# Prompt attention of a hybrid decoder step: values stationary, scaled probabilities, output by feature, and the order of scaling and maximum

## The reference

```
s = q . k * SCALE, masked;  p = softmax(s);  o_branch = p @ v          (for each of the 3 branches)
attn = g0 * o_compressed + g1 * o_selected + g2 * o_window             (gates g per row, branch and head)
merged = concat(rmsnorm(o_rnn) * gn_rnn, rmsnorm(attn) * gn_attn)      (rmsnorm over 512 features)
x = x + mods2 * (merged @ w_out);  then norm, SwiGLU feed-forward, norm
```

## Time and profile before

| | |
|---|---|
| Median of three timed runs | 1877.02 us (1874.16 to 1878.92) |
| Profiled execution, its own time | 1875.1 us |
| Its span in the trace | 1873.3 us |
| TensorE busy (weight loads) | 1721.3 us (1546.4) |
| VectorE busy | 938.1 us |
| ScalarE busy | 751.4 us |
| Mean granted clock of TensorE | 0.94 |

### The profile page before, as it was taken

The page is one execution under the profiler, slowest core; times in us unless marked ns, Lnnn a source line. Parts: engine busy times, 40 slices in busy tenths (PEclk is TensorE's granted clock), DMA queues, the critical chain, the costliest instruction groups (busy, mean ns, idle before and its releaser), DMA issues. The chain is left out here.

```text
span 1873.3 us, 30402 instructions
## 1 busy us (share of the span) xinstructions
PE 1721.3 (92%) x11011; PEld 1546.4 (83%) x11011; DVE 938.1 (50%) x1733; ACT 751.4 (40%) x1187; POOL 302.1 (16%) x303
## 2 busy tenths in 40 slices
PE   6999979799969899897679979999999999999998
PEld 3988945478859787785459979999999999999997
DVE  3647662344466666674555724443445443444433
ACT  3435501134446555462333435432235432345322
POOL 1100033311030000000015503003305013100032
PEclk7999989989979898898789989999999999999999
DMA  8355320164300000104525555544554544555443
GB/s 288 108 147 169 92 73 23 59 197 144 111 6 2 1 1 0 51 0 197 226 58 155 145 167 135 137 112 139 152 138 132 155 125 134 153 135 152 127 140 93
DMA packets 297157, 214.47 MB, mean 114 GB/s; under 512 B 20382, under 2 KB 284366, under 8 KB 293807
## 3 DMA queue, kind: packets, MB, share of 16 engines
q1 hardware_dynamic: 290412, 172.61, 32.3%
q0 software_dynamic: 4816, 40.73, 5.8%
q10 hardware_dynamic: 1842, 0.05, 0.1%
HBM read 206.07 MB, written 11.41 MB: 116 GB/s over the span
## 5 line engine op out<-in xcount | busy, mean ns | idle before, releaser
L423 DVE TENSOR_TENSOR ff_lo<-ff_raw,ff_hi 128x2048 fp32r<-128x2048 f32 (+1 forms) x126 | 265.6, 2108 | 220.1 <-ACT ff_hi L419 220.1
L428 PE MATMUL banks<-low_rows,ff_hi 128*128 128x352 f32 x1120 | 360.2, 322 | 0.0
L427 PE MATMUL banks<-ff_h_hi,ff_hi 128*128 128x352 f32 x1056 | 342.8, 325 | 12.3 <-DVE ff_lo L423 12.3
L429 PE MATMUL banks<-ff_h_hi,ff_lo 128*128 128x352 f32 x1056 | 340.1, 322 | 0.0
L419 ACT ACTIVATE ff_hi<-ff_raw 128x2048 fp32r<-128x2048 f32 (+1 forms) x126 | 215.4, 1710 | 235.5 <-PE banks L429 220.2
L428 PEld LDWEIGHTS banks<-low_rows,ff_hi 128*128 128x128 f32 x1120 | 211.5, 189 | 0.3
L427 PEld LDWEIGHTS banks<-ff_h_hi,ff_hi 128*128 128x128 f32 x1056 | 199.0, 188 | 13.6 <-issue 13.4
L429 PEld LDWEIGHTS banks<-ff_h_hi,ff_lo 128*128 128x128 f32 x1056 | 199.5, 189 | 0.0
L427 PE MATMUL banks<-hid_hi,ff_hi 128*128 128x352 f32 x528 | 171.9, 326 | 4.4 <-DVE hid_lo L423 4.1
L429 PE MATMUL banks<-hid_hi,ff_lo 128*128 128x352 f32 x528 | 170.6, 323 | 0.0
L428 PE MATMUL banks<-hid_lo,ff_hi 128*128 128x352 f32 x528 | 170.1, 322 | 0.0
(11 more groups left out here) (414 smaller groups left out, 3155.2 us busy)
## 6 DMA issues: line engine op xcount, KB each, us to landing
ff_raw<-in_w_gate SPq DMA_DIRECT2D x66, 512.0 KB, 4.0
ff_raw<-in_w_up SPq DMA_DIRECT2D x66, 512.0 KB, 5.2
ff_raw<-in_w_down SPq DMA_DIRECT2D x48, 384.0 KB, 4.1
late_ada<-in_w_ada SPq DMA_DIRECT2D x16, 1024.0 KB, 5.7
ff_raw<-in_w_down SPq DMA_DIRECT2D x48, 320.0 KB, 3.4
ff_raw<-in_w_out SPq DMA_DIRECT2D x24, 512.0 KB, 5.3
s_raw<-in_w_in SPq DMA_DIRECT2D x48, 128.0 KB, 2.6
streams<-in_x_prompt SPq DMA_DIRECT2D x4, 1024.0 KB, 9.3
```

The costliest lines, as they stand in the source:

```text
L423: return dve.tensor_tensor(lo, raw, hi.bitcast(F32), ALU.subtract)
L427: pe.matmul(out, lhsT=w_hi, rhs=x_hi, start=first, stop=False)
L428: pe.matmul(out, lhsT=w_hi, rhs=x_lo, start=False, stop=False)
L429: return pe.matmul(out, lhsT=w_lo, rhs=x_hi, start=False, stop=last)
```

## The change

- Value products: the values are stationary (64 weight columns), the turned probabilities of 128 rows move. The two key heads' products go to partitions 0 to 63 and 64 to 127 of one PSUM bank. Both branches and the compressed branch accumulate in the same bank.
- For that the probabilities are multiplied by gate over row sum before they are turned (`weigh`), in place, on VectorE. The merges go.
- ScalarE evicts a row tile's sum, features on the partitions, into `attnT` (`take`, two instructions for each row tile and trip).
- VectorE's order in step n is `weigh(n-1)`, `top(n)`, `copy(n-2)`.
- The four trips are one written-out sequence of 128 units; the next trip's staging, compressed scores and gates are issued between units of the trip before. The unit order in a row tile is branch, then key head.
- Four buffers of turned probabilities in place of two.
- GpSimd squares and sums the output by feature in trips 1 and 3; TensorE sums over features. The decode attention loses the squares and the scaling of the rows; it gets eight products of the identity with the row rates. The trunk spreads the rates by eight matmuls, VectorE scales `attnT` with gain and rate, and the turns of eight row tiles go. The output projection takes the gated stream's chunks first, attention's behind.

The core of the diff:

```diff
@@ prompt_attention, VectorE
-                def top(u):                       # step u: top(u), copy(u - 2), merge(u - 3)
-                def merge(u):
-                    t, h, br = units[u]
-                    j = slice(u % 4, u % 4 + 1)
-                    dve.wait_ge(probs_ready, i * U + u + 1)
-                    s.then(dve.reciprocal(coef[:, j], den[:, j]))
-                    s.then(dve.tensor_tensor(coef[:, j], coef[:, j], gsel[:, t, br, h:h + 1], ALU.mult))
-                    dve.wait_ge(out_summed, i * U + u + 1)
-                    dve.scalar_tensor_tensor(out, ps[6 + u % 2][:, 0:HEAD_DIM], coef[:, j], out, ALU.mult, ALU.add
-                                             ).then_inc(merged, 1)
+            def weigh(n):
+                i, t, br, h = order[n]
+                j = slice(n % 4, n % 4 + 1)
+                w = len(tiles_of[n]) * P
+                dve.wait_ge(probs_ready, n + 1)
+                s.then(dve.reciprocal(coef[:, j], den[:, j]))
+                s.then(dve.tensor_tensor(coef[:, j], coef[:, j], gsel[i % 2][:, t, br, h:h + 1], ALU.mult))
+                dve.tensor_scalar(probs[n % 2][:, 0:w], probs[n % 2][:, 0:w], coef[:, j], None, ALU.mult).then_inc(scaled, 1)
+            for n in range(1, DONE):
+                i, u = trip_of(n)
+                if n - 1 < N:
+                    weigh(n - 1)
+                if n < N:
+                    top(n)
+                if 0 <= n - 2 < N:
+                    copy(n - 2)
+                if i + 1 < KA:
+                    if u == SHIFT_AT:             # 4
+                        compress_shift(i + 1)
+                        pick_gates(i + 1)
+                    if u == PROBS_AT:             # 6
+                        compress_weigh(i + 1)
+                    if u == COPY_AT:              # 10
+                        compress_copy(i + 1)
+                    if u == FIRST_HALF_AT:        # 19
+                        stage(i + 1, 0)
+                if 0 < i < KA and u == SECOND_HALF_AT:   # 3
+                    stage(i, 1)
@@ prompt_attention, ScalarE
+            def exp(n):
+                act.wait_ge(max_ready, n + 1)
+                if n >= 2:
+                    act.wait_ge(turned0, n - 1)
+                    if second[n - 2]:
+                        act.wait_ge(turned1, upto[n - 2])
+                w = len(tiles_of[n]) * P
+                if n >= 4:
+                    act.wait_ge(scaled, n - 3)
+                act.activation(probs[n % 2][:, 0:w], psum[:, place[n]:place[n] + w], ACT.Exp,
+                               bias=nmax[:, n % 4:n % 4 + 1], accum_out=den[:, n % 4:n % 4 + 1]).then_inc(probs_ready, 1)
+            def take(v):
+                i, t, _, _ = order[2 * v]
+                act.wait_ge(out_summed, v + 1)
+                for h in range(N_KV):
+                    head = i + h * GROUP
+                    act.activation(attnT[own[head % 2], head // 2, t * P:(t + 1) * P], ps[6 + t % 2][own[h], 0:P], ACT.Copy
+                                   ).then_inc(taken, 1)
@@ prompt_attention, TensorE (turn(n) now waits for scaled instead of probs_ready)
-                        m = pe.matmul(ps[6 + u % 2][:, 0:HEAD_DIM], lhsT=pT[u % 2][:, j * P:(j + 1) * P],
-                                      rhs=kvn[:, kt, col:col + HEAD_DIM], start=(j == 0), stop=(j == len(tiles_of[u]) - 1))
+                for j, kt in enumerate(tiles):
+                    for h in range(N_KV):
+                        col = 2 * KV_WIDTH * br + KV_WIDTH + h * HEAD_DIM
+                        m = pe.matmul(bank[own[h], 0:P], lhsT=kvn[:, kt, col:col + HEAD_DIM], rhs=pT[(2 * v + h) % 4][:, j, :],
+                                      start=False, stop=(br == 2 and j == len(tiles) - 1), skip_group_check=True)
+            for n in range(2, DONE):              # step n: qk(n), turn(n - 2), weighted((n - 4) // 2) if n is even
@@ sample_attention, group 0
-                    for t in range(TILES):
-                        s.then(act.activation(win[:, 0:ATTN_WIDTH], attn[:, t, :], ACT.Square, accum_out=attn_sum[:, t:t + 1]))
-                    for t in range(TILES):
-                        s.done(dve.scalar_tensor_tensor(attn[:, t, :], attn[:, t, :], attn_sum[:, t:t + 1], gain_row, ALU.mult, ALU.mult))
@@ sample_attention, group 1
+                    for t in range(TILES):
+                        s.done(dve.tensor_scalar(rate_rows[:, t, :], ident[:, :], attn_sum[:, t:t + 1], None, ALU.mult))
@@ trunk
-            for t in range(4):
-                turn(t)
+            for t in range(TILES):
+                m = pe.matmul(ps[RATE_BANKS[t // 4]][:, t % 4 * P:(t % 4 + 1) * P], lhsT=ones[:, :], rhs=rate_rows[:, t, :], start=True, stop=True)
+            def scale(g):                         # VectorE: g = 0 first of all, 1 and 2 between the blocks
+                dve.wait_ge(rates_spread, 1)
+                ...
+                            m = dve.scalar_tensor_tensor(rows, rows, V["gn_attn"][:, c:c + 1], ps[RATE_BANKS[x // 512]][:, x % 512:x % 512 + y - x],
+                                                         ALU.mult, ALU.mult)
```

More of the change, by code:

```diff
@@ L1324, in prompt_attention @@
     second = [len(x) > 4 for x in tiles_of]
-    upto = [sum(second[:u + 1]) for u in range(U)]
-    C1 = upto[-1]
-    HT = TILES // 2
+    upto = [sum(second[:u + 1]) for u in range(N)]
+    HQ = SEQ // 2
+    DONE = N + 4
+    CMP_AT, SHIFT_AT, EXP_AT, PROBS_AT, TURN_AT, COPY_AT = 3, 4, 4, 6, 9, 10
+    FIRST_HALF_AT = PER // 2 + 3
+    SECOND_HALF_AT = 3
     with ExitStack() as st:
@@ L1489, in _, with double @@
+            for t in range(TILES):
+                pe.wait_ge(squared, t + 1)
+                m = pe.matmul(ps[4][:, 2 * t:2 * t + 2], lhsT=acc[:, t * P:(t + 1) * P], rhs=ones[:, 0:2], start=True, stop=True)
+            m.then_inc(rows_summed, 1)
         @block.scalar
         def _(act):
+            def double(i, half):
+                cols = slice(half * HQ, (half + 1) * HQ)
+                for h in range(N_KV):
+                    act.wait_ge(q_hi_done, (i * 2 + half) * N_KV + h + 1)
+                    act.activation(QD[h][own[1 - h], cols], QD[h][own[h], cols].bitcast(F32), ACT.Copy).then_inc(q_doubled, 1)
@@ new lines, in _ @@
+            double(0, 0)
+            compress_exp(0)
+            double(0, 1)
+            for n in range(DONE + 1):
+                i, u = trip_of(n)
+                if 0 <= n - 2 < N:
+                    copy(n - 2)
+                if n < N:
+                    exp(n)
+                if n < N and u == EXP_AT and i + 1 < KA:
+                    compress_exp(i + 1)
+                if n < N and u == FIRST_HALF_AT and i + 1 < KA:
+                    double(i + 1, 0)
+                if n < N and u == SECOND_HALF_AT and i:
+                    double(i, 1)
+                if n % 2 == 1 and n >= 5 and order[n - 5][2] == 2:
+                    take((n - 5) // 2)
@@ new lines, in _ @@
+            s.then(dve.memset(ck_pair[:, :, :], 0.0))
+            for h in range(N_KV):
+                s.done(dve.memset(QL[h][own[1 - h], :].bitcast(F32), 0.0))
+                s.done(dve.tensor_scalar(ck_pair[own[h], h, :], ck_p[own[h], :], SCALE, None, ALU.mult))
+            s.fence()
+            dve.wait_ge(masks_loaded, 48)
+            for dst, src in ((diag_b, diag), (tail_b, tail), (ident_b, ident)):
+                dve.tensor_copy(dst[:, :], src[:, :]).then_inc(masks_cast, 1)
+            stage(0, 0)
@@ L2421, in _ @@
             hi(0, 2, 8, 2 * KD)
-            for p in order[8:]:
-                part(p)
+            part(NG)
             hi(0, 2, 9, 2 * KD)
@@ L2556, in _ @@
                 dve.sem_inc(sem, 2)
+            scale(0)
             lo(0, 2, 0, 2 * KD)
-            for p in order[0:5]:
-                part(p)
+            part(0)
+            scale(1)
             lo(0, 2, 1, 2 * KD)
@@ L2571, in _ @@
             lo(0, 2, 5, 2 * KD)
-            part(order[7])
+            part(2)
             take(4)
```

469 lines of the change are left out of this document (234 added, 235 removed).

## The result

The changed kernel takes 1887.39 us, the median of five runs (1881.05 to 1891.71); the kernel before took 1875.50 beside it (1873.85 to 1878.92, five runs). The forecast had put the change at 21 us above the kernel before (1898 against 1877); it is 12. The profiled execution is the longest of the five: 1891.71 us with a span of 1889.9, against a span of 1873.3 before.

A forecast was written before the change was run, and what follows sets the result against it. TensorE bounded the old steady part, waits the trip borders; afterwards a closed VectorE-ScalarE chain would bound the prompt attention. 1875.1 + 26.9 (stage) - 6 (decode attention) + 0 (trunk) = 1896.0, with 1.9 carried over 1898 us; range 1881 to 1920.

The forecast's parts named there:

- the ring: Prompt attention, VectorE and ScalarE: maximum, exponential, scaling, next maximum as one closed chain, 317.8 us over 128 units.
- start of the chain: Prompt attention's first maximum: same VectorE work before or just behind it, so the chain begins where it did, 546.3.
- gap from maximum to exponential: Handover from VectorE's maximum to ScalarE's exponential in each unit: fixed 0.15 us, from 0.16 in the earlier trace.
- all else from maximum to maximum: Work laid into the chain: next trips' preparation 15.2 us, GpSimd's squares touching VectorE 1 us (0 to 6).
- decode attention: Row scaling gone, second group starts 8.7 us sooner, gather takes part back: 6 us saved (3 to 8.7).
- trunk: Start of the trunk: up to 2 us later, fewer turns give back up to 2; zero, within 2.
- rival A: Prompt attention: chain shorter per unit than summed, level at 0.17 us less, 1860 at 0.3 less; chance 0.12.
- Preparation: Between units on VectorE: shift and gates, weighing, staging in halves; 5.1 us unhidden, three times, 15.2 us.
- TensorE's work: Prompt attention: some 60 us of value products leave; about 50 us a trip remain, 65 at the dear bound.
- rival C: Value products not side by side: 232 ns a pair, TensorE 65 us a trip, time unchanged; no chance of its own.
- Rival B: Prompt attention: TensorE's clock falls through short rests and TensorE becomes the bound, 1930 us; chance 0.13.
- The carry-over: Whole kernel: timed runs' median lay 1.9 us above the profiled run; added again, 1896.0 becomes 1898.

The follow-up runs named there:

- no_scaling: Changed kernel without VectorE's scaling of the probabilities, the turn waiting for the coefficient instead (output lacks gate and normalisation): 1832.6 us, ratio 0.9772.
- before_act_unrolled: Kernel before, with ScalarE's prompt-attention program written out in place of its hardware loop over the trips: 1875.5 us, ratio 1.0004.
- both_orders: Changed kernel with VectorE's next maximum ahead of the scaling and TensorE's value products behind the next scores, ahead of the turn: 1832.2 us, ratio 0.9770.
- the edit alone: Kernel before, without squares and scaling of seven of the eight prompt row tiles in the decode attention: 1871.2 us, ratio 0.9984.

## Why the prediction was right, and where its sizes were off

By its own sum, in us:

| step | forecast | measured |
|---|---|---|
| the ring sets the pace | yes | yes: waits and timeline; no_scaling -54.8 |
| start of the chain | 546.3 | 544.8 |
| gap from maximum to exponential, 128 times | 0.15 each, 19.2 | 0.03 in 124 of them, as 128: 3.8, so 15.4 too many |
| all else from maximum to maximum (preparation, GpSimd) | 16.2 | 22.8 |
| from the last scaling to the stage's end | 5 | 7.1 |
| end of the stage | 885.3 | 877.1 |
| decode attention | -6 | -5.5 |
| trunk | 0 | +3.4 |
| own time | 1896.0 | 1891.7 |

The sum comes out near partly by luck: the gap and the start are 16.9 us too many, the four rows that were too small are 12.6 too few, and 4.3 remain.

- **The mechanism.** The exponential's wait, the maximum behind it in VectorE's queue, and TensorE falling off the path: all as forecast. The durations were right: the scaling in place takes 0.55 us at 640 keys (from the earlier trace rows: 0.552), the steps from accumulator to scaling 0.43 (forecast 0.42), the next maximum starts 0.08 before the scaling ends.
- **The mis-sized term.** The gap of the earlier trace rows was not the price of handing over from VectorE to ScalarE. In the widest units it belonged to ScalarE's hardware loop, as before_act_unrolled shows; at 640 keys 0.06 of the 0.17 did, and the 0.11 that stay there come with ScalarE's copy just ahead of the exponential; and 0.15 was not true of all units even before, where the gaps sum to 16.6 us and not to 19.2. The changed kernel has no loop, and there ScalarE's copy has ended 0.47 us or more before the exponential starts, so the unit of 640 keys takes 2.63 us, not 2.75. This 0.12 per unit is in rival A's place; rival A needed 0.17 to be level. I read the price of a gap from a row without asking which part of the program around it would stay.
- **Preparation.** The 15.2 us of the twelve preparations came true: above the ring, shift and gates cost 3.1 (forecast 3.9), weighing 2.3 (2.7), the two halves of staging 4.5 and 5.3 (3.9 and 4.8). The scaling beside GpSimd's squares takes no longer (at 640 keys 0.55 in all 40 units), so the 1 us for GpSimd isn't seen. The surplus is 4.0 us at the start: I put the first staging "before or just behind" the first maximum and counted none of it, but 2.75 us of VectorE's work lie between that maximum and its scaling (544.97 to 547.72), and the fifth maximum, at 554.38, waits 1.73 for its scores. Another 3.2 us lie in the first two units of the three later trips, where at 629.53 the maximum waits 0.35 for scores behind 32 value products of the trip before: apart from the start the only place where TensorE is still on the path. The last 0.4 us are spread.
- **TensorE's work.** I said 50 us a trip: 65 of steady part less 15. That left out what TensorE does around the border. Busy time before is 290 us in the stage (546 to 858), 72 a trip; in both_orders, where TensorE is nearly full, it is 256 us (541 to 817), 64 a trip. In the changed kernel TensorE is busy 0.85 of the time, not the 0.6 to 0.75 that I gave as a sign. It did no harm to the forecast, since the ring is longer still; it is why no_scaling and both_orders fell short of what I expected of them. The price of a pair was good: groups of 20, 24 and 28 products of 64 weight columns take 1.31, 1.53 and 1.75 us, 0.055 each, 0.11 a pair (forecast 0.116). In the group at 596.93 they start two at a time, 7 ns apart, and the next two 0.11 later, so rival C, not side by side, is false. These counts, as those of the prediction, are of trace records: each product instruction of the kernel stands as two, so the 1056 are 528 instructions.
- **Rival B.** The clock did fall at times. It is 0.50 to 0.66 in the first 25 us, where before 550 to 570 had 0.94; then 1.00 from 567 to 638, and 0.50 in four stretches behind, 639 to 649, 676.5 to 679.5, 721 to 731 and 803 to 809, which make the window means of 0.90 to 0.96. From 676.5 to 679.5 that is in wide units, the sign that I had named for being wrong. It cost nothing there: the maxima of 768 keys start at 674.22 and 677.15, the next one at 680.09, 2.93 and 2.94 apart, which is the ring of 768 keys with 0.03 for the gap (2.94). TensorE had room, so rival B is false in what it needs, that TensorE becomes the bound. The Trainium skill's page "TensorE: Matmul & The Clock Gate", section "A second HAM failure mode: psum-queue depth-cycling", would have had the clock swing under such rests. The trace agrees in part: with TensorE idle for 7.4 of the 50 us from 570 to 620 it stayed at 1.00, and later it swung.
- **Decode and trunk.** The gather takes part of the 9.02 us back, both in the changed kernel and with the edit alone. The trunk's 3.4 were given as 0 within 2: 2.7 of them are the later first product, 0.7 stay open. I named GpSimd as late as the old start, not that it would collide with VectorE's subtraction.
- **The carry-over.** I added 1.9 us for the median. The profiled execution after lies 4.3 above its median, so of the 10.6 us between forecast and median 4.3 are steps, and the rest, 1.9 + 4.3, is this.

So the change is slower since it takes some 60 us of work off TensorE, which was the bound, and puts a ring of two engines in its place that makes the stage 18 us longer. Each half of its gain needs its own order: maximum ahead of scaling (32 us), value products behind scores (23 more).

## What to carry to other kernels

When work moves onto an engine that alternates with another, write down the ring of waits that each engine's queue order closes, and sum it before you count the engine that gets lighter. Once you open a ring, look for the next one through the third engine's queue, and count that engine's work over a whole period, borders included: the gain ends at whichever comes first. A gap read from the trace belongs to the program around it; ask whether that part stays.

## What the hardware showed that was not expected

- ScalarE's exponential of 768 to 1024 keys started 0.17 us behind its releaser under a hardware loop whose waits are counted with the loop's register; with the same program written out, 0.03. At 256 keys, where it has fewer waits, it was 0.03 to 0.04 in both.
- VectorE's subtraction of two SBUF operands (128x2048) takes 2.29 us alone and 4.35 with 2.2 us of overlap with GpSimd's (128x1408, 3.17 us), which started first; where VectorE started first it took 2.29 and GpSimd's 4.01. The later one pays about the overlap. The Trainium skill's page "SBUF — State Buffer", section "Who interferes with whom", says that a VectorE instruction with two inputs in SBUF contends with a GpSimd one that reads SBUF, and that the order of issue decides who blocks; both orders seen here agree.
